# An encoder's mixing stage rewritten: attention without its turned copies, mLSTM masks on TensorE, S5 over four tokens

## The reference, cut to what matters

```python
for l in range(2):
    x = layer_norm(ALPHA*x + 0.5*swiglu_1(x))
    x = layer_norm(ALPHA*x + mix(x))               # the stage that changes
    x = layer_norm(ALPHA*x + cross_attention(x, mem))
    x = layer_norm(ALPHA*x + 0.5*swiglu_2(x))
def mix(x):
    dq, dk, dv, mq, mk, mv, mo, mi, mf, su = split_columns(x @ w_in)
    # four heads, two maps each: softmax(rope(q) rope(k)^T / 8), block-causal over 64 tokens
    a = p[:, :, 0] - lam * p[:, :, 1];  a_out = rms_norm(a @ dv)
    # mLSTM: q, k = silu(conv4(mq, mk)); a causal decay matrix exp(log_d - m) times q k^T, times v
    # S5: 16 groups of 64 complex states, x_t = lam_bar * x_(t-1) + B u_t;  y = gelu(Re(C x) + D u), GLU
    return concat([a_out, b_out, c_out]) @ w_out
```

## Time and profile before

| | |
|---|---|
| median of 3 runs | 1377.72 us (1377.54 to 1380.18) |
| profiled execution, its own time | 1376.7 us |
| its span | 1374.9 us, mean granted TensorE clock 0.959 |
| PE busy | 1264.1 us (92%) |
| DVE, ACT, POOL busy | 812.4, 578.1, 192.8 us |
| mixing stage, layer 0 / layer 1 | 193.3 / 176.5 us, PE busy 162.3 / 143.6 us |

### The profile page before, as it was taken

One profiled execution on the slowest core, in us unless ns is written; L12 is line 12 of the kernel. 1 busy time (PEld: TensorE's weight loads), 2 busy tenths in 40 slices (PEclk: granted clock), 3 DMA queues, 4 the chain that ended last, 5 costly groups with the idle time before them and its releaser, 6 DMA issues.

```text
span 1374.9 us, 15895 instructions
## 1 busy us (share of the span) xinstructions
PE 1264.1 (92%) x6568; PEld 1068.6 (78%) x6568; DVE 812.4 (59%) x1130; ACT 578.1 (42%) x656; POOL 192.8 (14%) x181
## 2 busy tenths in 40 slices
PE   6999999989669999999999999999875999799997
PEld 5788888878558888888887888888754887688885
DVE  5578556593675556444566785465937736544454
ACT  4444444425433535444443444444263335444441
POOL 1018000372000000000010180003720000000000
PEclk9999999999789999999999999999976999899999
DMA  8655555433024365555547555544211434455551
GB/s 282 236 184 184 184 184 163 144 123 123 31 92 158 128 204 184 184 188 192 192 148 270 186 184 184 184 151 156 92 61 62 139 118 143 152 184 186 190 193 43
DMA packets 155911, 219.52 MB, mean 160 GB/s; under 512 B 6816, under 2 KB 127776, under 8 KB 155840
## 3 DMA queue, kind: packets, MB, share of 16 engines
q1 hardware_dynamic: 152448, 205.61, 44.9%
q0 software_dynamic: 3120, 11.85, 2.4%
q10 hardware_dynamic: 272, 1.05, 0.2%
HBM read 217.44 MB, written 1.05 MB: 159 GB/s over the span
## 4 chain that ended last, share of the span: by engine, by line
PE 65%; issue 16%; DVE 11%; ACT 3%; POOL 2%; DMA 1%; SPq 0%; DVEq 0%; POOLq 0%
PE PS L469 20%; PE PS L470 19%; PE PS L471 19%; DVE WL L1376 3%; ACT WH L1043 1%; PE PS L500 1%; DMA RAW<-in_ffn_w_up 1%; DVE COUT L1560 1%; DVE ZS L1548 1%; PE PS L964 1%; PE PS L988 1%; ACT XH L1043 1%; PE PS L537 1%; POOL RO L1997 1%; ACT PR L1160 1%
## 5 line engine op out<-in xcount | busy, mean ns | idle before, releaser
L1376 DVE TENSOR_TENSOR WL<-RAW,WH 128x2048 fp32r<-128x2048 f32 (+1 forms) x198 | 445.3, 2253 | 272.4 <-ACT WH L1043 272.3
L1043 ACT ACTIVATE WH<-RAW 128x2048 fp32r<-128x2048 f32 (+1 forms) x198 | 370.5, 1877 | 148.4 <-DMA RAW<-in_ffn_w_up 128.5
L469 PE MATMUL PS<-WH,XH 128*128 128x512 f32 x832 | 333.4, 401 | 24.6 <-DVE WL L1376 9.4
L470 PE MATMUL PS<-WL,XH 128*128 128x512 f32 x832 | 327.5, 394 | 0.0
L471 PE MATMUL PS<-WH,XL 128*128 128x512 f32 x832 | 327.0, 393 | 0.0
L469 PEld LDWEIGHTS PS<-WH,XH 128*128 128x128 f32 x832 | 158.2, 190 | 59.0 <-DVE WL L1376 9.9
L471 PEld LDWEIGHTS PS<-WH,XL 128*128 128x128 f32 x832 | 158.2, 190 | 33.8
L470 PEld LDWEIGHTS PS<-WL,XH 128*128 128x128 f32 x832 | 158.4, 190 | 31.0
L469 PE MATMUL PS<-WH,HH 128*128 128x512 f32 x352 | 138.6, 394 | 5.7 <-issue 5.7
L470 PE MATMUL PS<-WL,HH 128*128 128x512 f32 x352 | 137.6, 391 | 0.0
L471 PE MATMUL PS<-WH,HL 128*128 128x512 f32 x352 | 137.6, 391 | 0.0
(11 more groups left out here) (312 smaller groups left out, 1805.5 us busy)
## 6 DMA issues: line engine op xcount, KB each, us to landing
RAW<-in_ffn_w_gate SPq DMA_DIRECT2D x88, 512.0 KB, 3.7
RAW<-in_ffn_w_up SPq DMA_DIRECT2D x88, 512.0 KB, 4.7
RAW<-in_ffn_w_down SPq DMA_DIRECT2D x88, 512.0 KB, 4.3
RAW<-in_w_in SPq DMA_DIRECT2D x44, 512.0 KB, 4.4
RAW<-in_xattn_wkv SPq DMA_DIRECT2D x32, 512.0 KB, 4.1
RAW<-in_xattn_wq SPq DMA_DIRECT2D x16, 512.0 KB, 4.4
RAW<-in_w_out SPq DMA_DIRECT2D x12, 512.0 KB, 4.0
RAW<-in_xattn_wo SPq DMA_DIRECT2D x12, 512.0 KB, 4.0
```

Of the source, the lines that this page charges most:

```text
L469: nc.tensor.matmul(out_ap, sh, mh, start=first, stop=False)
L470: nc.tensor.matmul(out_ap, sh, ml, start=False, stop=False)
L1043: return nc.scalar.activation(dst, src, ACT.Copy)
L1376: return v.tensor_tensor(dst, full, hi.bitcast(F32), ALU.subtract)
```

## The change

All of it is in the mixing stage and in what prepares it.
- S5 takes four tokens a step, so 64 steps. `s5_in` makes all four bands in a row, each from four taps with N = 64; the scans run over 256 elements (two per half instead of four of 128); VectorE turns the states back itself. `s5_out` has four taps with N = 63. `s5_turn` runs three times and `s5_taps` is twice as wide, in the first FFN; GpSimd's `scale_c` has 49 operations instead of 25.
- Queries and keys are made with the features on the partitions. The rotation is a copy (ScalarE, XE), a matmul by a permutation (`swap_halves`, 128 x 512) and three operations on VectorE (`rope`); GpSimd's rotation and `turn_q` go.
- The attention's mask is a matmul of one row in the score tile. Both maps are exponentiated from PSUM, both transposed (six transposes, not three), both multiplied with the values and a column of ones, whose sums divide the results afterwards.
- mLSTM: the first tap of the convolution is ScalarE's, from PSUM; the triangle is added by TensorE in `spread`; the inverse roots are a power on GpSimd.
- The order on all engines and the order of the units are new.

```diff
-        order += [(l, "DQ", 0), (l, "DQ", 1), (l, "SU", 0), (l, "MQ", 0), (l, "MK", 0), (l, "DK", 0), (l, "DK", 1),
-                  (l, "DV", 0), (l, "DV", 1), (l, "MM", 0), (l, "MM", 1)]
+        order += [(l, "DV", 0), (l, "DV", 1), (l, "DQ", 0), (l, "DK", 0), (l, "SU", 0), (l, "MQ", 0), (l, "MK", 0),
+                  (l, "DQ", 1), (l, "DK", 1), (l, "MM", 0), (l, "MM", 1)]
...
+            def s5_in(l):
+                pe.wait_ge(ut_ready.sem, ut_ready.at(l, 1))
+                for j in range(BANDS):
...
+                            for tap in range(TAPS):
+                                w = PAR[r:r + 32, P_B + o:P_B + o + P] if tap == TAPS - 1 else PBT[r:r + 32, 2 - tap, o:o + P]
+                                mm = nc.tensor.matmul(out_ap, w, UT[r:r + 32, f, tap * STEPS:tap * STEPS + STEPS],
+                                                      start=(tap == 0), stop=(tap == TAPS - 1))
...
+                        for tap in range(TAPS):
+                            o = f * SEQ + tap * STEPS
+                            for part in range(2):
+                                mm = nc.tensor.matmul(PS[r:r + 32, 2, o + 1:o + STEPS], CQ[:, 1 + tap, part, 4 * f + j, :],
+                                                      ZW[:, b, part, q * STEPS:q * STEPS + STEPS - 1],
+                                                      start=False, stop=True, skip_group_check=True)
...
+                nc.tensor.matmul(bank(b), kst[:, K_SWAP:K_SWAP + P], XE[:, :, :].rearrange("p h n -> p (h n)"),
+                                 start=True, stop=True).then_inc(swap_done.sem, 1)
...
+                        mm = nc.tensor.matmul(PS[:, b + m, q0 + k1 - 64:q0 + k1], kst[r:r + 1, K_EARLY:K_EARLY + P],
+                                              kst[r:r + 1, K_FAR:K_FAR + 64], start=False, stop=True,
+                                              skip_group_check=True)
...
+                for m in range(2):
+                    nc.tensor.matmul(PS[:, b + m, 0:129], AT[:, m, 0:P], DV[:, 0, h, :], start=True, stop=True)
...
+                        nc.tensor.matmul(PS[:, i, hh * SEQ:hh * SEQ + SEQ], pick, R_MAX, start=True, stop=False,
+                                         skip_group_check=True)
+                        nc.tensor.matmul(PS[:, i, hh * SEQ:hh * SEQ + P], ident, tri, start=False, stop=True,
+                                         skip_group_check=True)
+                        nc.tensor.matmul(PS[:, 3, h * P:h * P + P], pick, R_MAX[:, P:SEQ], start=True, stop=False)
+                        mm = nc.tensor.matmul(PS[:, 3, h * P:h * P + P], ident, tri, start=False, stop=True)
...
+            def s5_states(l, b):
...
+                v.tensor_tensor(z, both, cos, ALU.mult)
+                v.tensor_tensor(ZT[:, :, :], both, sin, ALU.mult).then_inc(bu_read.sem, 1)
+                dve.wait_ge(bu_read.sem, bu_read.at(l, b + 1))
+                v.tensor_tensor(z[:, 0, :], z[:, 0, :], ZT[:, 1, :], ALU.add)
+                link(v.tensor_tensor(z[:, 1, :], z[:, 1, :], ZT[:, 0, :], ALU.subtract))
+                for part in range(2):
+                    ins = v.tensor_tensor_scan(ZS[:, part, :], rad, z[:, part, :], 0.0, ALU.mult, ALU.add)
+                link(ins)
+                v.tensor_tensor(z, ZS[:, :, :], cos, ALU.mult)
...
-                m, q = SM[:, 160 + 4 * i:164 + 4 * i], SM[:, 168 + 4 * i:172 + 4 * i]
-                link(v.tensor_scalar(m, m, 1.0 / P, EPS, ALU.mult, ALU.add))
-                rsqrt(q, m, 4, 48)
```

More of the change, by code:

```diff
@@ L422, in load_ffn, with load_fill @@
                 load_down(l, s, FFN_UNITS - 1, BLOCKS - 1)
-            def load_fill(where, l):
-                for kl, kind, i in FILL[where, l]:
+            def load_fill(where, l, first=0, last=None):
+                for kl, kind, i in FILL[where, l][first:last]:
                     load_cols(UNIT[kl, kind, i], wkv_v, kl, 256 * i + (D if kind == "V" else 0))
@@ L577, in ffn @@
                     rows_product(b + 4 + 3 * j, [0, 1], HH, HL, False, False)
-                    if s == 0 and j == 6:
-                        s5_turn(l)
-                    if s == 0 and j == 7:
-                        s5_taps(l)
+                    if s == 0 and 6 <= j <= 8:
+                        s5_turn(l, j - 6)
                 j = BLOCKS - 2
@@ L588, in ffn @@
                 h_turned(l, s, j)
+                if s == 0:
+                    s5_taps(l)
                 unit_ready(b + 4 + 3 * j)
@@ L831, in mix, with mid @@
+            def mid(l, i, b):
+                if i < len(FILL["mid", l]):
+                    memory_unit(FILL["mid", l][i], b)
             def mix(l):
@@ L1195, in boundary, with mid_out, mid_split @@
                     split()
+            def mid_out(l, i, b):
+                if i < len(FILL["mid", l]):
+                    kv_out(FILL["mid", l][i], b)
+            def mid_split(l, i):
+                if i < len(FILL["mid", l]):
+                    split()
             def mix(l):
@@ L1275, in mix @@
+                copy(CH[:, 6:8, :].rearrange("p f (k s) -> p f k s", s=TAPS),
+                     UT[:, :, :].rearrange("p f (s k) -> p f k s", s=TAPS)).then_inc(c_hi.sem, 1)
+                split()
+                diff_turned(l, 2)
+                mid_out(l, 1, 3)
+                mid_split(l, 3)
+                diff_evac(l, 2)
+                diff_exp(l, 3)
                 split()
-                if FILL["mid", l]:
-                    kv_out(FILL["mid", l][3], 0)
-                diff_evac(l, 1)
@@ new lines, in mix @@
+                rope(l, 0)
+                split()
+                rope(l, 1)
+                split()
+                split()
+                diff_max(l, 0)
+                s5_states(l, 0)
+                gates_in(l)
+                s5_states(l, 1)
+                split()
+                conv(l, 0)
+                mid_split(l, 0)
+                rope(l, 2)
+                gates_out(l)
+                conv(l, 1)
+                dve.wait_ge(km_used.sem, km_used.at(l, 1))
+                v.memset(VA[:, :, :, 64:65], 1.0).then_inc(va_ones.sem, 1)
@@ new lines, in mix @@
+                mid_split(l, 1)
+                diff_sums(l, 0)
+                diff_combine(l, 0)
+                rope(l, 3)
+                split()
+                diff_max(l, 1)
+                diff_max(l, 2)
+                split()
+                mid_split(l, 2)
+                dve.wait_ge(glu_sig.sem, glu_sig.at(l, 1))
+                v.tensor_tensor(UT[:, :, :], ZG[:, :, :], UT[:, :, :], ALU.mult).then_inc(c_hi_in.sem, 1)
+                gate_scale(l)
+                diff_sums(l, 1)
```

1033 lines of the change are left out of this document (485 added, 548 removed).

## The result

The changed kernel took 1461.48 us (median of 4 runs, 1455.57 to 1466.21) beside 1377.91 for the kernel before on the same chip: a ratio of 1.060, 95% interval 1.056 to 1.064. It is 84 us slower, where I forecast 13 us faster, and far outside my range of 1346 to 1379. The profiled execution of the changed kernel took 1455.57 us, that of the kernel before 1376.7.

A forecast was written before the change was run, and what follows sets the result against it. Bound: TensorE's in-order program and, where it stops, VectorE and ScalarE behind each other. Layer 0 -10.6, layer 1 -8.8, FFN +6.6 sum to -12.8, from 1376.7 to 1363.9 us, 1365 as median; range 1346 to 1379.

The forecast's parts named there:

- none of these waits is as long as the 8.5 us one, so I leave 1.5 and 4 us instead of 16 and 20: Mixing stages of layers 0 and 1: half-clock time falls to 1.5 and 4 us, from up to 16 and 20.
- The masks of diff_scores: 16 matmuls, 32 records with weights 128 wide: +3.6: TensorE, attention scores: the mask matmuls add 3.6 us a layer.
- spread: 2560 columns instead of 1024, twice 0.91 ns each: +2.8: TensorE, spread: more columns at 0.91 ns, two records each, add 2.8 us a layer.
- 166.2 and 143.7: TensorE's work at full clock in layers 0 and 1: 146 and 123.5 us, plus 20.2 added a layer.
- no wait for a transfer stands in TensorE's list now: SP's reordered loads: each starts when the unit five before is used; no cost counted for them.
- 2.5 before mlstm_num: Layer 0: TensorE waits 2.5 us before mlstm_num, for combine and then decay_scores.
- 1.6 for cat_lo: Layer 0: TensorE waits 1.6 us for cat_lo.
- the rival in which short matmuls stream freely: s5_in at 58 ns a record saves 7.0 us a layer, the masks 1.7: 1348 us; chance 0.15.
- the rival in which weight loads floor it: s5_out: 128 records at 112 instead of 50 ns, +8 us a layer: 1381 us; chance 0.08.
- The ES waits: Kernel before: transposes of the attention probabilities wait 16.8 us in three waits for VectorE's combination (ES).
- my signs of an error: Forecast wrong if a stage has a wait over 5 us, GpSimd's coefficients are waited for, or s5_in takes 7 us.
- The slow end of my range was carried by waits: Rival: waits move without shrinking, VectorE's chain and the tail taking 7 us a layer more: about 1379 us; chance 0.14.

The follow-up runs named there:

- Runs 3: Every s5_in matmul streams 128 columns instead of 64, S5 result altered, against the changed kernel: 1460.22 us, ratio 1.060.
- run 10: As Run 9, but s5_in's 128 rows come from copies of UT with zeros in the other 96, keeping the changed kernel's sums: 1378.57 us, ratio 0.9998.
- run 1: s5_in's 128 records cut into 16 pieces of 8, one behind every 6 products of MQ and MK, against the changed kernel: 1501.73 us, ratio 1.088.
- run 8: Changed kernel with 64-row masks and 128 rows in s5_in (S5 result altered), spread and gateT: 1394.68 us, ratio 1.012.
- run 12: On run 10's kernel, two more splits (third and fourth mid units) moved later in layer 0: 1369.46 us, ratio 0.9929.
- Run 2: Mask matmuls take 64 rows of constants instead of one, like the scores, against the changed kernel: 1427.31 us, ratio 1.036.
- run 6: On Run 2's kernel, spread's matmuls that pick a gate row take all 128 rows, in the old order: 1414.3 us, ratio 1.025.
- Run 9: On run 8's kernel, two splits moved later on ScalarE and VectorE (fourth unit from mid, first behind W): 1377.22 us, ratio 0.9987.
- run 11: The changed kernel with Run 9's two later splits alone: 1447.39 us, ratio 1.050.
- run 7: On Run 2's kernel, s5_in's four bands of 32 records set apart, with other TensorE work between them: 1446.68 us, ratio 1.047.
- run 4: Every s5_in matmul takes all 128 rows instead of its band's 32, S5 result altered, against the changed kernel: 1441.29 us, ratio 1.046.

## Why the prediction was wrong

**The step that failed first** is the one on half clock: "none of these waits is as long as the 8.5 us one, so I leave 1.5 and 4 us instead of 16 and 20". I tied the clock to waits, because in the windows of before the low clock and the waits share a stretch. It measured 35.3 and 33.6 us, and the first fall came in the middle of work without a gap. The rule was not empty: 12 of layer 0's 35 us begin at waits. But it had nothing for the rest. In the kernel before s5_in came as 16 records of 32 rows, 2 us, with 5.8 to 12 us of wide products between. The change makes one run of 128 records out of it, and I counted that as price times number. Runs 3 and 4 tie the fall in s5_in to the rows in use and not to the columns, run 10 shows that zeros in the other rows keep the clock, run 1 that mixing finely does not. Filled rows and equal tiles together took half clock down to 12.4 and 10.7 us (run 8), the later splits to 5.2 and 6.0 (run 12). The Trainium skill's "TensorE: Matmul & The Clock Gate", Part 1, has the gate go by how busy the engine has recently been. The falls at the waits of 7.5 and 2.4 us agree with it; the first fall does not, since ahead of it TensorE is busy 4.79 of 4.79 us in the profile.

**The second** is a price in the sum: "The masks of diff_scores: 16 matmuls, 32 records with weights 128 wide: +3.6" and "spread: 2560 columns instead of 1024, twice 0.91 ns each: +2.8". Both took rows of runs of one tile, where the change has tiles of 64 rows and 1 row, and of 4 rows and 128, in turn. Measured: a head's scores 3.5 us at full clock and up to 6.2 at half, 18.1 us for the four in layer 0; spread 11.8 us in layer 0. Run 2 took 34 us off by giving both the same 64 rows, and run 6 another 13 in spread. Part of both gains is the clock: head 2's scores and much of spread had run at half. The work at full clock then comes out at 166.9 and 143.8 us in run 12; I had 166.2 and 143.7. That this agrees to a percent is in part luck, since it has 64-row masks that cost 43 ns where I had 112. Its 1369.5 us lie 4 us above the forecast of 1365, with the three causes taken out.

**The third** is "no wait for a transfer stands in TensorE's list now", with "2.5 before mlstm_num" and "1.6 for cat_lo". No wait of TensorE names a transfer in the kernel after either: it is handed on through the in-order queues of ScalarE and VectorE. In the kernel after these waits are 7.5 and 5.3 us. The load of the mid unit starts at the use of the unit five before it, which was stated, but I did not lay it against the place of its split. Run 9 gave 17 us for moving two splits, run 11 14 us.

**What was right.** s5_in costs 112 ns a record at full clock; the rival in which short matmuls stream freely (1348) is out. s5_out costs 3.45 / 64 = 54 ns, I had 50, so the rival in which weight loads floor it is out as well. The first FFN became 3.1 us longer (3.3 forecast) and GpSimd's coefficients are not waited for. PE waits 1.0 us for the end of the convolution (1.5) and 1.2 for the swaps (1.1). The ES waits are gone. Of my signs of an error, a wait of over 5 us came true three times: 18.8 us in all against the 7.1 I had for the three, which alone would have eaten 12 of the 13 us and not turned the sign.

**The chances.** The slow end of my range was carried by waits, and the only rival slower than the kernel before was a floor under s5_out. No case had the clock in it as a loss, though the prediction's own rows gave the old stages 36 us of half clock. The range could not hold what no rival named.

## What to carry to other kernels

A run of matmuls with few rows is to be priced twice, at full and at half clock, and so is the wide work next to it. If the operands allow zeros in the other rows, fill them: a record cost the same 112 ns, and the clock held here. Weights of different row counts are not to be put in turn: equal rows took a mask addition from 180 to 43 ns. And where a split or copy in an in-order engine needs a load, its earliest landing (here the use of the unit five before, plus load and two casts, 11 us in run 8) is to be laid against its place in the queue before a wait is called covered.

## What the runs showed of the hardware that was not expected

- The granted clock fell from 1.00 to 0.52 after 4.8 us of records of 32 rows by 64 columns, and after 4.3 us with 128 columns, with TensorE busy throughout. It stayed at 1.00 for 14.33 us with 128 rows by 64 columns, at the same 112 ns a record, and so with zeros in 96 rows of the moving operand. The time to the fall is not one number: 2 us into the second band in run 7, 3.0 us in run 1, and 1 us of 8-row records behind the 128-row run in run 4.
- Six products of 256 columns on 128 rows, between groups of eight 32-row records, ran at the 1.2 GHz level for the whole 20.8 us shown of run 1. Where 48 of them followed one band of 3.7 us, in run 7, the clock stayed at 1.00.
- With all rows of spread in use (run 6) the clock fell 0.8 us behind a wait of 3.2 us and was full again after 3.1 us of 128-row records.
- At full clock, 64-row and 1-row weights in turn cost 205 and 180 ns a record; 64-row weights in both, with the two halves of the rows in turn, cost 80 and 43 ns.
